# A two-layer attention trunk: value products in two column groups, denominators from sums of probability tiles

## What is computed

```python
def attend(q, keys, vals, scale):
    s = jnp.einsum('bqhgd,bkhd->bhgqk', q, keys) * scale
    p = jax.nn.softmax(s.astype(jnp.float32), axis=-1).astype(vals.dtype)
    return jnp.einsum('bhgqk,bkhe->bqhge', p, vals)

def latent_attention(q, k, v, k_c, v_c, scale):      # 512 latent queries, 768 keys
    keys = jnp.concatenate([k_c, k], axis=1)
    vals = jnp.concatenate([v_c, v], axis=1)
    ...
y  = latent_attention(q, k, v, kc, vc, scale).reshape(z.shape) * jax.nn.silu(z)
yc = attend(qc, kc, vc, scale).reshape(zc.shape) * jax.nn.silu(zc) if want_ctx else None
```

## Time and profile before

| | us |
|---|---|
| median of 3 runs | 985.08 (984.52 to 987.39) |
| the profiled execution, as timed | 984.78 |
| its span on the core | 982.7 |
| granted TensorE clock, mean | 0.985 |

### The profile page before, as it was taken

One profiled execution on the slowest core, in us unless ns is written; L12 is line 12 of the kernel. 1 busy time (PEld: TensorE's weight loads), 2 busy tenths in 40 slices (PEclk: granted clock), 3 DMA queues, 4 the chain that ended last, 5 costly groups with the idle time before them and its releaser, 6 DMA issues.

```text
span 982.7 us, 12419 instructions
## 1 busy us (share of the span) xinstructions
PE 932.3 (95%) x4483; PEld 654.1 (67%) x4483; DVE 486.6 (50%) x829; ACT 427.2 (43%) x779; POOL 168.4 (17%) x198
## 2 busy tenths in 40 slices
PE   3899999999999999999999889999999999999996
PEld 3588889888555555555588678789785545445584
DVE  4456443532455555655524562743544565555524
ACT  5435443321454445466821432643314435456712
POOL 1110001000632222002161200001016321002150
PEclk9999999999999999999999889999999999999999
DMA  9741220410402222031035202220404000022032
GB/s 345 266 113 31 77 65 1 107 44 2 171 1 91 82 88 83 1 110 63 1 135 126 86 23 64 76 74 1 128 23 171 1 1 0 1 86 87 0 108 85
DMA packets 67865, 74.16 MB, mean 75 GB/s; under 512 B 6148, under 2 KB 47456, under 8 KB 67680
## 3 DMA queue, kind: packets, MB, share of 16 engines
q1 hardware_dynamic: 61392, 60.23, 19.4%
q0 software_dynamic: 4016, 12.77, 3.7%
q10 hardware_dynamic: 2400, 0.38, 0.2%
HBM read 69.18 MB, written 4.19 MB: 75 GB/s over the span
## 4 chain that ended last, share of the span: by engine, by line
PE 88%; DVE 5%; ACT 3%; issue 2%; ACTq 1%; POOL 0%; DVEq 0%
PE pv L1741 12%; PE bank L1529 9%; PE bank L1530 9%; PE bank L1531 9%; PE bank L1785 7%; PE bank L1824 4%; PE bank L1823 4%; PE bank L1822 4%; PE bank L1702 4%; PE bank L1669 3%; PE bank L1789 2%; PE bank L1636 2%; PE bank L1572 2%; PE bank L1571 2%; PE bank L1573 2%
## 5 line engine op out<-in xcount | busy, mean ns | idle before, releaser
L1529 PE MATMUL bank<-hA_parts,W_parts 128*128 128x512 f32 (+1 forms) x496 | 180.8, 365 | 7.8 <-DVE h_low_parts L1084 5.9
L1530 PE MATMUL bank<-hA_parts,W_parts 128*128 128x512 f32 (+1 forms) x496 | 174.5, 352 | 0.0
L950 ACT ACTIVATE hA<-bank 128x512 f32<-128x512 f32 (+1 forms) x168 | 93.2, 562 | 102.3 <-PE bank L1785 77.8
L1365 DVE TENSOR_REDUCE mxp<-bank 128x1 f32<-128x384 f32 x192 | 96.6, 551 | 49.5 <-PE bank L1702 49.1
L1529 PEld LDWEIGHTS bank<-hA_parts,W_parts 128*128 128x128 f32 x496 | 95.1, 192 | 26.7 <-issue 10.8
L1531 PE MATMUL bank<-h_low_parts,W_parts 128*128 128x512 f32 (+1 forms) x310 | 109.0, 352 | 0.0
L1530 PEld LDWEIGHTS bank<-hA_parts,W_parts 128*128 128x128 f32 x496 | 95.2, 192 | 13.2 <-issue 1.9
L1741 PE MATMUL pv<-hA,vg 128*128 128x512 f32 (+1 forms) x168 | 81.8, 572 | 4.4 <-ACT hA L950 4.2
L1741 PE MATMUL pv<-hA,h_low 128*128 128x512 f32 (+1 forms) x144 | 69.5, 564 | 0.0
L1091 DVE TENSOR_TENSOR W_parts<-W,W_parts 128x1024 fp32r<-128x1024 f32 x44 | 53.5, 1221 | 28.5 <-ACT W_parts L672 28.2
L1531 PEld LDWEIGHTS bank<-h_low_parts,W_parts 128*128 128x128 f32 x310 | 59.3, 191 | 8.0
(11 more groups left out here) (269 smaller groups left out, 1807.0 us busy)
## 6 DMA issues: line engine op xcount, KB each, us to landing
W<-in_w_in SPq DMA_DIRECT2D x39, 512.0 KB, 4.0
W<-in_w_mod SPq DMA_DIRECT2D x8, 2048.0 KB, 8.0
W<-in_w_out SPq DMA_DIRECT2D x4, 2048.0 KB, 7.8
gqk<-in_w_mod SPq DMA_DIRECT2D x2, 1536.0 KB, 9.4
cqkv<-in_w_mod SPq DMA_DIRECT2D x2, 1536.0 KB, 13.8
XA<-in_x SPq DMA_DIRECT2D x4, 512.0 KB, 7.2
XA<-in_x POOLq DMA_DIRECT2D x4, 512.0 KB, 6.9
x_between_layers<-XA POOLq DMA_DIRECT2D x4, 512.0 KB, 2.9
```

What stands on the lines that cost most here:

```text
L950: act.activation(prob[slot % 4][:, 0:nq], ps("sc", l, h, q0, kt)[:, 0:nq], ACT.Exp, scale=MLA_SCALE if h < MLA_H else GQA_SCALE)\
L1365: dve.tensor_reduce(mxp[:, t, half:half + 1], ps("mx", l, h, q0, t, half)[:, 0:384], AX, ALU.max).then_inc(*up("part_max", l, h, q0, t, half))
L1529: pe.matmul(p[:, 0:c[1]], high[:, k, :], h_hi[:, k, toks], start=(k == 0), stop=False)
L1530: pe.matmul(p[:, 0:c[1]], low[:, k, :], h_hi[:, k, toks], start=False, stop=False)
```

## The change

1. `vm` and `vg` hold the 64 value columns alone. A unit's value product becomes two, each with the 64 value columns as weights: half of the queries into partitions 0 to 63 of the bank, the other half into 64 to 127, each of half the columns.
2. The denominators come from sums of `prob` tiles. POOL adds the two context tiles, and tiles 0+1, 2+3 and the sum of both of the latent group (`add_pair`, `both_sums`); DVE adds tiles 4+5 (`last_pair`, after the next head's maxima). `den(h-1)` multiplies these sums with ones, in two column groups, after the `nm` transposes and the key projection of head h, in a bank of the ring; for the last head after the first output tile's first half.
3. There are six `prob` buffers, and `flush(most, keep_n)` acts only when `most` products are pending: in the middle of a head at six (layer 0) or five (layer 1), down to two, and all that are left before the `nm` transposes. One `pv` bank serves a whole head.
4. `recip` runs once per head over 128 partitions and 384 (layer 0) or 256 columns; `normalise` runs for both query groups in the next head, its first step in two halves.
5. The loads of `x_back` are issued by SP, before the load of the output weights, and wait for head 5. The low weights on POOL are spread over heads 9 to 11, between the adds. The ones in `vm` and `vg` are no longer written.

```diff
+PROBS = 6
-        vg = sb("vg", [P, TILES, 2, 192])
+        vg = sb("vg", [P, TILES, 2, 64])
+        pair_sum = {0: [sums[:, 512:768]], 256: [sums[:, 0:512], last_sum[:]]}
 # SP
+                    if i == W_POS[("out", l, 0)]:
+                        sp.wait_ge(*at("prob_used", l, slot_of(l, MLA_H - 1, 256) + 5))
...
+                            sp.dma_start(X[:, t, :], src).then_inc(*dma("x_back", l))
 # POOL
+                def add_pair(h, q0, nq, i):
+                    slot, to = slot_of(l, h, q0) + 2 * i, min(i, 1)
+                    pool.wait_ge(*at("prob", l, slot + 1))
+                    if head_before(l, h, 1):
+                        pool.wait_ge(*at("filled", "den", *head_before(l, h, 1)))
+                    pool.tensor_tensor(pair_sum[q0][to], prob[slot % PROBS][:, 0:nq],
+                                       prob[(slot + 1) % PROBS][:, 0:nq], ALU.add).then_inc(*up("pair_sum", l, h, q0, i))
...
+                    add_pair(h, *qbs(l)[-1][:2], 0)
+                    if 3 * (h - 9) in range(KD):
+                        low_weights(0, (3 * (h - 9),))
+                    add_pair(h, *qbs(l)[-1][:2], 1)
+                    if 3 * (h - 9) + 1 in range(KD):
+                        low_weights(0, (3 * (h - 9) + 1,))
+                    pool.wait_ge(*at("pair_sum", l, h, 256, 1))
+                    pool.tensor_tensor(pair_sum[256][0], pair_sum[256][0], pair_sum[256][1], ALU.add)\
+                        .then_inc(*up("both_sums", l, h))
 # ACT
+                def recip(h):
+                    n = sum(nq // 2 for _, nq, _ in qbs(l))
+                    act.wait_ge(*at("filled", "den", l, h))
+                    act.activation(rd[:, 0:n], ps("den", l, h)[:, 0:n], ACT.Ln).then_inc(*up("den_ln", l, h))
+                    act.activation(rd[:, 0:n], rd[:, 0:n], ACT.Exp, scale=-1.0).then_inc(*up("recip", l, h))
...
-                        if slot >= 4:
-                            act.wait_ge(*at(*prob_reader(l, slot - 4)))
+                        if slot >= PROBS:
+                            act.wait_ge(*at("prob_used", l, slot - PROBS))
+                            act.wait_ge(*at(*added(l, slot - PROBS)))
 # DVE
+                    for e in range(2):
+                        half = slice(64 * e, 64 * e + 64)
+                        dve.scalar_tensor_tensor(out=un[r:r + 64, n2 * e:n2 * e + n2], in0=pv_banks[h % 2][half, cols],
+                                                 scalar=0.5, in1=rd[half, cols], op0=ALU.mult, op1=ALU.mult)\
...
+                def last_pair(h):
+                    slot = slot_of(l, h, 256) + 4
+                    dve.wait_ge(*at("both_sums", l, h))
+                    dve.wait_ge(*at("prob", l, slot + 1))
+                    dve.tensor_tensor(pair_sum[256][1], prob[slot % PROBS], prob[(slot + 1) % PROBS], ALU.add)\
+                        .then_inc(*up("last_sum", l, h))
...
                     if h + 1 < len(heads):
-                        maxima(h + 1, tile, h)
-                    elif len(qbs(l)) == 2:
-                        normalise(h, *qbs(l)[0][:2])
+                        maxima(h + 1, tile)
+                    last_pair(h)
 
                 y_low(range(4))
 # PE
+                    v = vm[kt][:, h, :] if h < MLA_H else vg[:, kt, (h - MLA_H) // 3, :]
+                    o, n2 = pv_banks[h % 2][:, half_cols(q0, nq)], nq // 2
+                    for e in range(2):
+                        mm = pe.matmul(o[64 * e:64 * e + 64], v, prob[sl % PROBS][:, n2 * e:n2 * e + n2],
+                                       start=(kt == 0), stop=(kt == nkt - 1), skip_group_check=True)
+                def den(h):
+                    p = open_("den", l, h)
...
+                            for e in range(2):
+                                mm = pe.matmul(p[64 * e:64 * e + 64, cols], ones[:, 0:64], part[:, n2 * e:n2 * e + n2],
+                                               start=(i == 0), stop=(i == len(parts) - 1), skip_group_check=True)
...
-                    flush(1)
+                    flush(1, 0)
                     max_rows(h)
                     if h + 1 < len(heads):
                         project_k(h + 1)
-                    flush(0)
+                    if h:
+                        den(h - 1)
...
-                        flush(2)
+                        flush(6 if l < DEPTH - 1 else 5, 2)
```

## The result

| | us |
|---|---|
| median with the change, 4 runs | 1006.20 (1003.49 to 1008.42) |
| before, 4 runs | 985.12 (984.52 to 987.39) |
| ratio, with its 95% interval | 1.021 (1.017 to 1.025) |
| the profiled execution with the change, as timed | 1008.38 (span 1006.5) |

A forecast was written before the change was run, and what follows sets the result against it. PE was taken to bound heads 0 to 4, with another engine often last in heads 6 to 10; -11.8 - 1.3 + 1.1 + 4 + 5.5 + 6.9 = +4.4 on 984.78 gave 989.2 us, range 971 to 1001.

The forecast's parts named there:

- the price of DVE's delays in the GQA heads: Heads 6 to 10, both layers: +1.1 us for DVE's longer chain and +4 for meetings with POOL's adds.
- heads 0 to 4: Both layers, PE's saving counts in full: -11.8 us; layer 0's heads 1 to 4 shorter by 1.03 each.
- PE's own sum: PE alone, whole kernel: values -67.1, `den` +23.3, ways in and out of column groups +21.6, together -22.2 us.
- two flushes and no `den`: Head 0 of layer 0: saving of 3.01 less 0.60 for the two flushes, -2.4 us.
- it holds if nothing becomes late: Condition on the -11.8 us of heads 0 to 4; ACT and DVE are busy under 60% there.
- in heads 0 to 5 PE covers them: DVE's meetings with POOL's adds, 0.4 to 0.9 us each, cost nothing in heads 0 to 5.
- the context group ahead of the maxima: In `normalise` of heads 6 to 10: split step, context part ahead of the low parts, +0.45 us.
- meetings with POOL: DVE steps beside POOL's adds: 0.4 us in each of ten GQA heads, +4 (bounds 0 and +9).
- The third rival: Clock falls inside GQA heads once PE waits about 2 us in one piece; 2 to 3 us each, 1001; chance 0.17.
- the main case: Whole kernel: the forecast of 989.2 us, by its bounds between 983 and 996; chance 0.45.
- The last heads: Output waits for `last_pair` behind POOL, PE idle about 4 us: +5.5 for both layers, clock 2.2 more each end.
- At nothing: Terms priced at zero: `x_back` loads and output weights, POOL's rounding of next keys, spread low weights, six `prob` buffers.

The follow-up runs named there:

- e2: The change with POOL's adds 8 columns wide instead of 512 or 256, order and waits unchanged (denominators not the reference's): 980.61 us, ratio 0.995.
- e4: The change with layer 0's context group normalised behind the context maxima, and the last head's low weights and last_pair moved later: 990.43 us, ratio 1.006.
- e0: The changed kernel itself, measured again beside the kernel before: 1006.97 us, ratio 1.021.
- e3: The change with, in the last head, POOL's low weights 6 and 7 behind its adds and last_pair behind the first four y_low: 998.30 us, ratio 1.013.
- e5: e4 with eight extra unused products of 128 columns ahead of the first maxima products of heads 5 and 6, both layers: 988.19 us, ratio 1.004.
- e8: e4 with POOL's adds of heads 5 to 10 waiting for the next head's low parts, last-head low weights for Y's: 982.60 us, ratio 0.999.
- e9: e8 with eight extra products of 128 columns ahead of the first maxima products of heads 5, both layers: 978.49 us, ratio 0.993.
- e10: e9 with the three low weights of heads 9 and 10 behind POOL's third add instead of between the adds: 975.28 us, ratio 0.991.
- e11: e10 with four extra products of 128 columns at each of two places in layer 0's head 6: 973.54 us, ratio 0.989.

## Why the prediction was right and wrong

The step that failed is the price of DVE's delays in the GQA heads, with the clock left out of them: +5.1 us for the ten heads 6 to 10, and they grew by 14.7 in the profile, falls included. That is 9.6 of the 19.4 us between forecast and profile; 6.2 more are heads 0 to 4, and 1.9 the stretch between the layers. The direction and the places of the delays were right.

**PE's own sum was right.** PE's timeline in layer 0, head 0 of the changed kernel:

```profile
282.77 1.08 PE L1759 MATMUL pv<-more,h_low 128*64 128x256 f32 x8
283.69 1.03 PE L1759 MATMUL pv<-hA,h_low 128*64 128x256 f32 x8
284.65 0.82 PE L1734 MATMUL bank<-con,nmx 128*1 128x128 f32 x6
```

Each row is two units of 512 columns: four units pass in 1.88 us, 0.43 each and 0.16 us for the way in. Heads 1 to 3 of layer 0 got shorter by 0.98, 0.97 and 0.97 us where 1.03 was worked out. The Trainium skill ("TensorEngine Tiling (Array Packing)", section "Key Properties") says that changing the tiling mode drains the engine. The trace agrees: each stretch costs time beyond its products, 0.16 us on the way in here.

**Heads 0 to 4 gave back half of it.** One step is plain: `den(0)` stands ahead of head 1's scores, so it lies in head 0's stretch, and "two flushes and no `den`" was wrong: 1.38 and 1.16 us. Then PE met waits that the value products had covered: 0.75 us in layer 0's head 0 and 0.3 in heads 1 and 2 of layer 1, for line 1271, and 1.0 in layer 1's head 3 for line 1296. I had written "it holds if nothing becomes late", and something did. The 1.0 us in head 3 is a meeting as well: with narrow adds (e2) the wait is gone and the head takes 15.7 us and not 16.6, so "in heads 0 to 5 PE covers them" was not right either. About 0.4 us in layer 0's head 0 and 1 us in layer 1 are not accounted for.

**Heads 6 to 10, the term that was mis-sized most.** The mechanisms were in the text (the context group ahead of the maxima, +0.45; meetings with POOL, +0.4 a head), and the places too. The sizes were wrong by nearly three. For the meetings alone e2 gives a measure: with narrow adds the ten heads took 14.0 us less than with the change, falls included, where +4 was forecast. A meeting cost 0.8 to 1.1 us for each step hit, two or three steps in a row were hit (head 9: +1.8; head 6 of layer 1: +3.0), and the wait was then not shared out but stood on PE in one piece of 2.2 us. I had the longest of line 1341 in hand, 1.59 us, and took a fraction of it, with no row that said how often. The Trainium skill ("SBUF — State Buffer", section "Who interferes with whom") calls contention of the two engines an exclusive lock. By it a step waits for POOL's operation, at most for the whole of it. The trace agrees: the steps grew from 0.55 to 1.63, 0.95 to 1.91 and 0.69 to 1.64 us, by 0.95 to 1.08 each, beside adds that take 1.27 alone. With that price a meeting would have stood at about 1 us and not at 0.4. What I should have counted is which steps of DVE stand beside an add in the new order: the adds start when the second exponential is there, which is just when DVE starts on `normalise` and the low parts.

**The clock.** The third rival, with 0.17, is what happened in layer 0: falls in heads 6, 7, 9 and 10, beside waits of 2.0, 2.7, 2.2 and 2.2 us. It had the right point ("about 2 us in one piece"), and its price of 2 to 3 lies between the two measured, 1.6 for 3.4 us at half speed and 3.1 for 6.8; the four falls were short ones. One reading under it was off: before, the longest wait of PE in those heads was 1.18 us, not under 1. I gave it too little because I put the waits under 1 us, from the same too small meetings. That the clock comes on top is shown by heads 5, where PE's work is the same and the clock is not: in layer 0, behind a wait of 2.75 us, 18.8 us without a fall (e4), 20.4 with one of 3.4 (e0) and 22.0 with one of 6.8 (the first profile); in layer 1, behind 2.16, 13.8 (e2), 15.5 (e3) and 17.1. The right forecast was the main case and this rival together: they aren't alternatives, the first leads to the second. In the profile of the change about 33 us more stand at half speed than before, and at 0.46 a us (3.1 by 6.8, e4 to e5) this is at most 15 of the 24 us; an estimate, since where PE waits anyway a low clock costs less.

**The last heads.** A wait "of about 4 us", a clock fall behind each, `den` in the output: 4.45 and 4.7 us, and in all +10.3 us where +9.9 was forecast. e3 confirms the cause.

**At nothing.** The loads of `x_back` and the output weights never appear among PE's waits, right. The stretch between the layers is 0.6 to 1.9 us longer in all kernels with the change. In the profile of the change 1.5 of the 1.9 us are more idle time of PE there, the largest piece 0.99 us at line 1616, which waits for ACT (0.15 before). Why ACT is later stays open.

## What to carry to other kernels

Work that is moved to an idle engine isn't free for its neighbour: list which steps of VectorE stand beside it, and price each one that reads SBUF tiles alone at nearly the other's whole duration (0.8 to 1.1 us beside 1.27 here), then place the moved work beside steps that read PSUM (e8: three steps 3.0 us shorter in one head for one wait). When an engine loses work that filled the gaps, its waits come together. Behind a wait of TensorE of 2.0 to 2.8 us the clock mostly fell here, for another 1.6 or 3.1 us; where such a wait was filled in heads 5 it didn't (e5, e9, e10, e11), and nothing was gained where it hadn't fallen before. Rivals of which one leads to the other are one case, and their prices add.

## What the hardware showed that I hadn't expected

- A cast with one SBUF input is hit too: line 1333 of e4 took 1.63 us, 0.55 in e8. POOL's adds also lengthen, from 1.28 to 1.98 us at most in head 9 of the change.
- The same kernel, in the same head, ran 3.4 us at half speed in one execution and 6.8 in another (e0 and the first profile), and the same wait of 2.75 us was followed by no fall in e4. And a fall needs no long wait: in e9 the clock fell at 903.7 us with waits of 1.28 and 1.03 us, two products apart, around it, and in e10 and e11 in layer 0's head 9 (448.6 and 448.4 us) with a single idle piece of PE in that head before it, of 0.80 us.
- Eight useless products of 0.24 us stood where a head got 3.1 us shorter (e5), as short as the head was without them when the clock stayed up (e2).
